# Chunk attention of the first block: heads taken in pairs, step by step, with the products spread between the steps

## Chip, cores and metric

The kernel runs on one core of a Trainium2 chip. The metric is the device time of one execution in microseconds (us), the median of the runs.

## What is computed

512 tokens of width 1024 pass through a block of two layers and then a second block. The part that matters here is the second layer of the first block, cut to its core:

```
hn = rms_norm(h, kv_norm_g)
k, v = hn @ w_k, hn @ w_v                      # 16 heads of 64
q = rms_norm(h, g[0]) @ w_q
s = einsum('bcqhd,bckhd->bchqk', q, k_band)    # 64-token chunks, own chunk and 8 before
s = s * (HEAD_DIM ** -0.5) + relative_bias(rel_table)
s = where(valid, s, NEG_INF)
p = softmax(s, axis=-1)
o = einsum('bchqk,bckhd->bcqhd', p, v_band)
m = o @ w_o
h = h + rms_norm(m, g[1])
```

With 512 tokens a query sees every earlier chunk and its own.

## The kernel before, in words

Activations stand feature-major, 8 tiles of 128 features by 512 tokens. Each weight matrix comes in units: 128 rows by 1024 columns, which are 8 tiles of 128x128, the weights of 128 output features. SyncE loads a unit into one of four slots of `RAW`. GpSimd splits it into a high part `WH` and a rest `WL` (L292, L295). Activations are split likewise (`XH`/`XL`, `HH`/`HL`). A tile of a product is then three matmuls (`three_passes`, L333 to L335), a product 24, and its result stands in one PSUM bank of 512 columns. The counts `weights_split`, `units_done` and `evacuated` order it: a unit waits for its split weights and a free bank, GpSimd for the slot, VectorE for the result.

The attention layer has 8 units for V, 16 for K and Q, 8 for the out product. V goes first, token-major. Then come four K/Q products (two of K, two of Q) for the first four heads, and four rounds of four heads.

In a round (`attention_round`, one on each engine) a block n is one head and one query tile t of 128 tokens, which needs 128(t+1) keys: n = 8a + 4hh + t for head hh of pair a. TensorE, at block n, does the scores of n (L463, K of 64 features, so 64 rows of the array), the transposes of the probabilities of n-2 (L473), the values of n-3 (L484, output to 64 partitions), and in the first three rounds, for n < 12, two tiles of one of the next round's K/Q products (`piece`). These are plain fp32 matmuls. VectorE adds the bias (L1192), takes the negated maximum (L1099), and later the reciprocal of the sum (L1105) and the scaling (L1106). ScalarE does the exponential with its sum (L733), copies the transposes out of PSUM (L744), and stages each round: it copies K, Q and V of the two pairs to `KP`, `QP` and `VP` (L799 to L801), since the rounds are a loop with register addresses and the next K and Q overwrite `KQ`. Outputs of a pair go to `VT` (L804).

Round 4 is the same without products. Then ScalarE copies the eight output tiles from `VT` to `HH` (L815), VectorE takes the rest into `HL` (L1209), and the eight out products run: three together, tile by tile as the parts come, then five.

The scores of block n stand in bank 4 + n % 2, the transposes in 6 + n % 2, the values of pair a in bank a, and K/Q products in banks 2 and 3.

Of the kernel before, what the change touches and what calls it, by code (L numbers as in the profile page):

```python
# [27 lines left out]
P = 128  # L28
SEQ = 512
D = 1024  # L30
# [87 lines left out]
def program(nc, xT, weights, gains, cols, lng, lnb, bs, wsT, rel, pos, ident_d, decay, pT, out):  # L118
    with ExitStack() as ctx:
# [31 lines left out]
        KQ = at("KQ", 152, [P, 4, SEQ])  # L151
        MGH = at("MGH", 144, [P, DT, SEQ], F32R)
# [11 lines left out]
        PTB = at("PTB", 194, [P, 2, SEQ])  # L164
        ROT = at("ROT", 188, [P, 4, SEQ])
# [57 lines left out]
        oh_ready = sem("att_high_ready")  # L223

# [82 lines left out]
        def _(pe):  # L307
# [224 lines left out]
            for xh, xl in ((XH, XL), (XH, XL), (HH, HL), (HH, HL)):  # L532
                product(DT, xh, xl)
            pe.wait_ge(evacuated, bank.now() + SLOTS)
            outs = Count(oh_ready)

            def first_round(ahead):
                attention_round(lambda a: KP[:, a, :], lambda a, hh, k: VP[:, a, k, hh * HD:hh * HD + HD],
                                outs, ahead)
            with loop(pe, 3, [(st, 2), (sr, 16), (pr, 16), (pt, 16), (outs, 2), (split, 4), (bank, 4)]) as i:  # L540
                first_round(((XH, XL), (HH, HL)))
            first_round(None)
            pe.wait_ge(oh_ready, outs.now())
            hr.next(DT)
            products(HH, HL, hr)
# [89 lines left out]
        def _(act):  # L635
# [36 lines left out]
            def branch_squares(first, tables=False):  # L672

                ev.n = SLOTS + first
                for t in range(DT):
                    act.wait_ge(evacuated, ev.next())
                    square(M[:, t, :])
# [106 lines left out]
            def load_bias(i, a):  # L784


                h = bass.ds(i * 4 + 2 * a, 2)
                to = slice(2 * a, 2 * a + 2)
                act.dma_start(BIAS[CH:P, to, :], rel[CH:P, h, :]).then_inc(in_bias[a], 16)
                act.dma_start(BIAS[0:CH, to, 0:SEQ - CH], rel[0:CH, h, 0:SEQ - CH]).then_inc(in_bias[a], 16)  # L790

            def pair_of(i, a):

                return VT[:, :, bass.ds(i * 256 + a * P, P)]

            def stage_pairs(i):
                act.wait_ge(evacuated, ev.next(4))
                for a in range(2):
                    S.activation(KP[:, a:a + 1, :], KQ[:, a:a + 1, :], ACT.Copy)  # L799
                    S.activation(QP[:, a:a + 1, :], KQ[:, 2 + a:3 + a, :], ACT.Copy)  # L800
                    S.activation(VP[:, a, :, :], pair_of(i, a), ACT.Copy).then_inc(staged, 1)  # L801

            def output(i, a):
                S.activation(pair_of(i, a), PS[:, a, :].rearrange("p (t n) -> p t n", t=TT), ACT.Copy)\  # L804
                 .then_inc(oh_ready, 1)
            load_bias(0, 0)
            load_bias(0, 1)
            ev.n = SLOTS + FIRST["att_kq"]
            with loop(act, 3, [(mx, 16), (td, 16), (pv, 16), (ev, 4)]) as i:
                attention_round(i, stage_pairs, output, lambda a: load_bias(i + 1, a))  # L810
            attention_round(3, stage_pairs, output)
            act.wait_ge(units_done, FIRST["att_out"] + SLOTS)
            act.wait_ge(oh_ready, DT)
            for f in range(DT):
                S.activation(HH[:, f, :].rearrange("p (t n) -> p t n", t=TT), VT[:, :, f * P:f * P + P], ACT.Copy)\  # L815
                 .then_inc(xh_ready, 1)
            branch_squares(FIRST["att_out"])
            stat()

            pre_norm([(G_FFN1, XH)], FIRST["ffn_a1"], hn)  # L820
# [102 lines left out]
        def _(dve):  # L923
# [265 lines left out]
            def add_bias(n, dst, src):  # L1189
                if n % 8 == 0:  # L1190
                    dve.wait_ge(in_bias[n // 8], bias_in[n // 8].next(32))
# [333 lines left out]
```

## Time and profile before

| | us |
|---|---|
| median of 3 runs | 2806.67 |
| lowest, highest | 2802.98, 2808.89 |
| span of the profiled execution | 2797.4 |
| TensorE matmul busy | 2563.7 (92%) |
| VectorE busy | 1393.3 (50%) |
| ScalarE busy | 545.4 (19%) |
| GpSimd busy | 1779.9 (64%) |
| mean granted TensorE clock | 0.936 |

The profile's own execution is known by its span, from the first to the last instruction; the times of the runs include what lies around it. A busy share is an average over stages: the attention layer is one stage among 17, so it is read by its own stretch, which runs from 635.5 to 937.0 us, with round 1 from 658.5, round 2 from 715.6, round 3 from 775.1, round 4 from 836.2 to 889.3, and then the out products. The granted clock is a share of 2.4 GHz: 1.00 is that level, 0.50 is 1.2 GHz. A time of a matmul in the timeline includes its way through the array, so its cost in a row of matmuls is read from start to start.

### The profile page before, as it was taken

What the parts mean: (1) busy time and instruction counts of PE and PEld (TensorE: products, weight loads), DVE (VectorE), ACT (ScalarE), POOL (GpSimd) and SP (SyncE); (2) the same over time, 40 slices, a digit from 0 to 9 for tenths busy, and PEclk for the clock granted to TensorE, in tenths of its full rate; (3) what the DMA queues carried; (4) which work ended last, traced back from release to release, by engine and by line L of the source; (5) the groups of instructions that cost most, each with busy time, mean ns of one, the idle gap of its engine ahead of it and who ended that gap; (6) DMA issues with size and microseconds to landing.
All of it is one profiled execution on the core that took longest, in us unless ns stands there. A gap on an engine that the chain in (4) does not pass through costs nothing.

```text
span 2797.4 us, 31291 instructions
## 1 busy us (share of the span) xinstructions
PE 2563.7 (92%) x10766; PEld 2002.8 (72%) x10766; DVE 1393.3 (50%) x1682; ACT 545.4 (19%) x972; POOL 1779.9 (64%) x827
## 2 busy tenths in 40 slices
PE   6789999979999799997899998788989998999987
PEld 5667888856555688886688886456567887888875
DVE  4665433563543634437633237789435237423366
ACT  2122110121332211111211012320322112101022
POOL 6657787845320687786588776464015877887865
PEclk9999999989996999999899999898579999999998
DMA  4222333322110233332233322122002332333322
GB/s 161 76 66 83 98 98 97 92 66 82 52 51 0 68 106 96 92 103 79 63 98 97 96 84 77 53 75 60 0 27 60 97 101 78 103 98 90 99 74 68
DMA packets 64795, 221.40 MB, mean 79 GB/s; under 512 B 7504, under 2 KB 9680, under 8 KB 64592
## 3 DMA queue, kind: packets, MB, share of 16 engines
q1 hardware_dynamic: 59184, 208.17, 25.3%
q10 hardware_dynamic: 5536, 12.19, 1.4%
q8 instruction: 52, 0.85, 0.1%
q14 instruction: 23, 0.19, 0.0%
HBM read 218.23 MB, written 2.10 MB: 79 GB/s over the span
## 4 chain that ended last, share of the span: by engine, by line
PE 77%; DVE 16%; issue 3%; ACT 2%; POOL 1%; ACTq 0%; DMA 0%; DVEq 0%; POOLq 0%
PE PS L333 21%; PE PS L334 21%; PE PS L335 21%; PE PS L403 3%; PE PS L463 3%; PE PS L484 3%; DVE SS L956 2%; DVE XL L964 2%; PE PS L473 2%; DVE RI L974 1%; PE PS L573 1%; POOL WH L292 1%; DVE T L985 1%; DVE MK L1279 1%; POOL WL L295 1%
## 5 line engine op out<-in xcount | busy, mean ns | idle before, releaser
L292 POOL TENSOR_TENSOR WH<-RAW,ONES 128x1024 fp32r<-128x1024 f32 (+3 forms) x411 | 791.2, 1925 | 959.0 <-PE PS L335 867.1
L295 POOL TENSOR_TENSOR WL<-RAW,WH 128x1024 fp32r<-128x1024 f32 (+3 forms) x411 | 993.5, 2417 | 32.3
L333 PE MATMUL PS<-XH,WH 128*128 128x512 f32 x1816 | 729.0, 401 | 80.6 <-DVE XL L964 27.6
L334 PE MATMUL PS<-XL,WH 128*128 128x512 f32 x1816 | 715.9, 394 | 0.0
L335 PE MATMUL PS<-XH,WL 128*128 128x512 f32 x1816 | 714.8, 394 | 0.0
L333 PEld LDWEIGHTS PS<-XH,WH 128*128 128x128 f32 x1816 | 347.0, 191 | 183.3 <-issue 71.1
L333 PE MATMUL PS<-HH,WH 128*128 128x512 f32 x1056 | 416.3, 394 | 13.7 <-DVE M L996 10.9
L334 PE MATMUL PS<-HL,WH 128*128 128x512 f32 x1056 | 413.2, 391 | 0.0
L335 PE MATMUL PS<-HH,WL 128*128 128x512 f32 x1056 | 413.0, 391 | 0.0
L335 PEld LDWEIGHTS PS<-XH,WL 128*128 128x128 f32 x1816 | 346.3, 191 | 74.1
L334 PEld LDWEIGHTS PS<-XL,WH 128*128 128x128 f32 x1816 | 347.0, 191 | 70.6 <-issue 1.4
L1010 DVE TENSOR_TENSOR HL<-T,HH 128x512 f32 x108 | 227.7, 2108 | 152.8 <-ACT HH L702 108.2
L333 PEld LDWEIGHTS PS<-HH,WH 128*128 128x128 f32 x1056 | 199.6, 189 | 60.0 <-issue 12.1
L335 PEld LDWEIGHTS PS<-HH,WL 128*128 128x128 f32 x1056 | 199.5, 189 | 42.1
L334 PEld LDWEIGHTS PS<-HL,WH 128*128 128x128 f32 x1056 | 199.6, 189 | 40.6
L1042 DVE TENSOR_TENSOR M<-PS,M 128x512 f32 x80 | 55.4, 692 | 329.7 <-PE PS L335 329.7
L699 ACT ACTIVATE T<-T 128x512 f32<-128x512 f32 x64 | 40.4, 632 | 496.9 <-DVE T L1017 496.9
L403 PE MATMUL PS<-WH,XH 128*128 128x512 f32 x192 | 83.7, 436 | 57.9 <-DVE XL L964 32.2
L956 DVE TENSOR_TENSOR SS<-SS,T 128x512 f32<-128x512 f32 x91 | 109.5, 1203 | 26.9 <-ACT T L658 26.9
L1027 DVE TENSOR_TENSOR T<-PS,RI 128x512 f32<-128x512 f32 x44 | 30.4, 690 | 182.9 <-PE PS L335 182.9
L964 DVE SCALAR_TENSOR_TENSOR XL<-H,GAIN,XH 128x512 fp32r<-128x512 f32 x64 | 92.4, 1444 | 0.0
L733 ACT ACTIVATE PB<-PB,NM 128x128 f32<-128x128 f32 (+1 forms) x96 | 53.9, 561 | 195.1 <-DVE NM L1099 194.6
(190 smaller groups left out, 2413.6 us busy)
## 6 DMA issues: line engine op xcount, KB each, us to landing
RAW<-in_weights SPq DMA_DIRECT2D x379, 512.0 KB, 3.5
RAW<-in_weights SPq DMA_DIRECT2D x16, 384.0 KB, 3.2
H<-in_xT ACTq DMA_DIRECT2D x8, 256.0 KB, 8.8
BIAS<-in_rel ACTq DMA_DIRECT2D x8, 256.0 KB, 3.4
RAW<-in_weights SPq DMA_DIRECT2D x8, 256.0 KB, 2.7
out<-R ACTq DMA_DIRECT2D x8, 256.0 KB, 2.1
BIAS<-in_rel ACTq DMA_DIRECT2D x8, 224.0 KB, 3.8
DECAY<-in_decay ACTq DMA_DIRECT2D x1, 1024.0 KB, 5.0
```

Of the source, the lines that this page charges most:

```text
L292: nc.gpsimd.tensor_tensor(WH[:, slot, 0:w], raw, ONES[:, 0:1].to_broadcast([P, w]), ALU.mult).then_inc(high_split, 1)
L295: nc.gpsimd.tensor_tensor(WL[:, slot, 0:w], raw, WH[:, slot, 0:w].bitcast(F32), ALU.subtract).then_inc(weights_split, 1)
L333: nc.tensor.matmul(PS[:, bank_, :], WH[:, slot, w], xh[:, k, :], start=(k == 0), stop=False)
L334: nc.tensor.matmul(PS[:, bank_, :], WH[:, slot, w], xl[:, k, :], start=False, stop=False)
L335: return nc.tensor.matmul(PS[:, bank_, :], WL[:, slot, w], xh[:, k, :], start=False, stop=stop)
L403: last = nc.tensor.matmul(PS[:, (first + j) % SLOTS, :], x[:, k, tok], wt[:, slot, w], start=(k == 0 and n == 0), stop=(k == DT - 1 and n ...
L463: nc.tensor.matmul(PS[:, 4 + n % 2, 0:n_of(t)], QP[r, a, t * P:t * P + P], k_of(a)[r, 0:n_of(t)], start=True, stop=True).then_inc(s_done, 1)
L473: last = nc.tensor.transpose(PS[:, 6 + n % 2, k * P:k * P + P], PB[:, n % 3, k * P:k * P + P], IDENT[:])
L484: last = nc.tensor.matmul(PS[hh * HD:hh * HD + HD, a, t * P:t * P + P], v_of(a, hh, k), PTB[:, n % 2, k * P:k * P + P], start=(k == 0), st ...
L956: V.tensor_tensor(SS[:], SS[:], T[:, slot, :], ALU.add).then_inc(ss_ready, 1)
L964: V.scalar_tensor_tensor(dl[:, t, :], H[:, t, :], gain(g, t), dh[:, t, :].bitcast(F32), ALU.mult, ALU.subtract).then_inc(ready, 1)
L1010: V.tensor_tensor(HL[:, f, :], T[:, src:src + 1, :], HH[:, f, :].bitcast(F32), ALU.subtract).then_inc(h_ready, 1)
```

## The change

The rounds and their loops go. 32 steps s = 4p + t are written out, each for both heads of pair p and query tile t. TensorE does the scores of step s, two tiles, the transposes of step s-1, two tiles, the values of step s-1. The tiles come from one list: the 16 K/Q units, ordered K, Q, K, Q by pair, then 21 tiles of the first three out units. 18 tiles stand ahead of step 0. K goes to bank 2 and Q to bank 3.

The staging copies go: scores read K and Q from `KQ`, which holds two pairs, and values read V from `VT`. VectorE adds the bias and takes the negated maximum in one `tensor_tensor_reduce`. A pair's output is split straight from PSUM: ScalarE writes the high part `OH`, VectorE the rest `OL`. The out product's result goes to `M2` in place of `M`, in banks shifted by two. `load_bias` is per pair.

```diff
+            def kq_tile(j):
+                n, k = kq0 + j // DT, j % DT
+                xh, xl = (XH, XL) if n % 2 == 0 else (HH, HL)
+                if k == 0:
+                    pe.wait_ge(weights_split, n + 1 + SLOTS)
+                    pe.wait_ge(evacuated, n + 3)
+                last = three_passes(2 + n % 2, n % SLOTS, slice(k * P, k * P + P), xh, xl, k, k == DT - 1)
...
+            def out_tile(j):
+                n, k = (out0 + j % 2, j // 2) if j < 2 * DT - 2 else (out0 + 2, j - 2 * DT + 2)
...
+                pe.wait_ge(o_low, k + 1)
+                out_high(n, k)
+                out_low(n, k)
...
+            def pair_scores(s):
+                p, t = divmod(s, TT)
+                if t == 0:
+                    pe.wait_ge(evacuated, kq0 + 2 * p + 2 + SLOTS)
+                if s:
+                    pe.wait_ge(x_done, 2 * s)
+                for hh in range(2):
+                    r = slice(hh * HD, hh * HD + HD)
+                    nc.tensor.matmul(PS[:, 4 + hh, 0:n_of(t)], KQ[r, 2 + p % 2, t * P:t * P + P],
+                                     KQ[r, p % 2, 0:n_of(t)], start=True, stop=True).then_inc(s_done2, 1)
+            def pair_transposes(s):
+                t = s % TT
+                for hh in range(2):
+                    pe.wait_ge(p_done, 2 * s + hh + 1)
+                    if s:
+                        pe.wait_ge(pt_done, 2 * s - 1 + hh)
+                    for k in range(t + 1):
+                        last = nc.tensor.transpose(PS[:, 6 + hh, k * P:k * P + P],
+                                                   PROB[:, s % 2, hh, k * P:k * P + P], IDENT[:])
...
+            def pair_values(s):
+                p, t = divmod(s, TT)
+                pe.wait_ge(pt_done, 2 * s + 2)
+                if t == 0 and p >= 2:
+                    pe.wait_ge(o_low, p - 1)
+                for k in range(t + 1):
+                    for hh in range(2):
+                        last = nc.tensor.matmul(PS[hh * HD:hh * HD + HD, p % 2, t * P:t * P + P],
+                                                VT[:, k, (2 * p + hh) * HD:(2 * p + hh) * HD + HD],
+                                                PROBT[:, hh, k * P:k * P + P], start=(k == 0), stop=(k == t))
...
+            for j in range(2 * DT + 2):
+                filler(j)
+            for s in range(steps + 1):
+                j = 2 * DT + 2 + 4 * s
+                if s < steps:
+                    pair_scores(s)
+                filler(j)
+                filler(j + 1)
+                if s:
+                    pair_transposes(s - 1)
+                filler(j + 2)
+                filler(j + 3)
+                if s:
+                    pair_values(s - 1)
+            pe.wait_ge(o_high, DT)
+            for n in range(out0, out0 + 3):
+                out_high(n, DT - 1)
+            pe.wait_ge(o_low, DT)
+            for n in range(out0, out0 + 3):
+                out_low(n, DT - 1).then_inc(units_done, 1)
...
+            def high_output(p):
+                act.wait_ge(pv_done2, 2 * TT * (p + 1))
+                S.activation(OH[:, p, :], PS[:, p % 2, :], ACT.Copy).then_inc(o_high, 1)
...
+            for s in range(DT * TT):
+                p, t = divmod(s, TT)
+                if t == 1 and p:
+                    high_output(p - 1)
+                if s:
+                    probs_out(s - 1)
+                for hh in range(2):
+                    c = s % 2 * 2 + hh
+                    act.wait_ge(x_done, 2 * s + hh + 1)
+                    x = PROB[:, s % 2, hh, 0:n_of(t)]
+                    S.activation(x, x, ACT.Exp, bias=NMX[:, c:c + 1], scale=-1.0,
+                                 accum_out=SUMX[:, c:c + 1]).then_inc(e_done, 1)
...
+            def low_output(p):
+                dve.wait_ge(o_high, p + 1)
+                t = slice(p * P, p * P + P)
+                V.tensor_tensor(OL[:, :, t], PS[:, p % 2, :].rearrange("p (t n) -> p t n", t=TT),
+                                OH[:, p, :].rearrange("p (t n) -> p t n", t=TT).bitcast(F32), ALU.subtract)\
+                 .then_inc(o_low, 1)
...
+                for hh in range(2):
+                    c = s % 2 * 2 + hh
+                    dve.wait_ge(s_done2, 2 * s + hh + 1)
+                    if s >= 2:
+                        dve.wait_ge(t_done2, 2 * s - 3 + hh)
+                    V.tensor_tensor_reduce(PROB[:, s % 2, hh, 0:n], PS[:, 4 + hh, 0:n],
+                                           BIAS[:, p % 2 * 2 + hh, SEQ - n:SEQ],
+                                           -1.0, 3e38, ALU.add, ALU.min, NMX[:, c:c + 1]).then_inc(x_done, 1)
+                if t == 1 and p < DT - 1:
+                    take_k(p + 1)
+                if t == 3 and p < DT - 1:
+                    take_q(p + 1)
+                if t == 1 and p:
+                    low_output(p - 1)
+                for hh in range(2):
+                    c = s % 2 * 2 + hh
+                    x = PROB[:, s % 2, hh, 0:n]
+                    dve.wait_ge(e_done, 2 * s + hh + 1)
+                    link(V.reciprocal(RECX[:, c:c + 1], SUMX[:, c:c + 1]))
+                    V.tensor_scalar(x, x, RECX[:, c:c + 1], None, ALU.mult).then_inc(p_done, 1)
```

How the instructions now stand. First TensorE, before: blocks 4 and 5 of round 1 (L463 scores, L473 transposes, L484 values, L333 to L335 a tile of a product).

```order
L463 MATMUL PS<-T 128x128 [waits scores_read]
L473 MATMUL PS<-IDENT,PB 128x128 [waits probs_t_ready,probs_ready]
L473 MATMUL PS<-IDENT,PB 128x128 x2
L484 MATMUL PS<-PTB,VP 64x128 [waits probs_t_ready]
L484 MATMUL PS<-PTB,VP 64x128
L341 REGISTER_ALU
L333 MATMUL PS<-HH,WH 128x512 [waits evacuated,weights_split]
```

TensorE in the change, steps 2 and 3 of pair 0 (L602 scores, L612 transposes, L623 values, L345 to L347 a tile).

```order
L623 MATMUL PS<-PROBT,VT 64x128 [waits pair_probs_t_ready]
L623 MATMUL PS<-PROBT,VT 64x128
L602 MATMUL PS<-KQ 128x384 [waits pair_biased]
L602 MATMUL PS<-KQ 128x384
L345 MATMUL PS<-HH,WH 128x512
```

```order
L612 MATMUL PS<-IDENT,PROB 128x128 [waits pair_probs_t_ready,pair_probs_ready]
L612 MATMUL PS<-IDENT,PROB 128x128
L612 MATMUL PS<-IDENT,PROB 128x128 [waits pair_probs_t_ready,pair_probs_ready]
L612 MATMUL PS<-IDENT,PROB 128x128
L345 MATMUL PS<-HH,WH 128x512
```

Scores, transposes and values of one head stood together between two pairs of tiles. Now values and scores stand together, each for two heads, and the transposes apart from them with a pair of tiles on either side.

VectorE in a round before, one block of 256 columns and the one behind it:

```order
L1192 TENSOR_TENSOR PB<-PS,BIAS 128x256 [waits probs_transposed,scores_done]
L1099 TENSOR_REDUCE NM<-PB 128x1 [waits scores_read]
L1105 RECIPROCAL REC<-SUM 128x1 [waits exp_done]
L935 REGISTER_ALU
L1106 TENSOR_SCALAR PB<-PB,REC 128x128 [waits dve_self]
```

and in the change, a step with t = 1 of the second pair (L1329 bias and maximum, L1302 K of the next pair, L1314 the rest of the pair before):

```order
L1329 ISA PROB,NMX<-PS,BIAS 128x256 [waits pair_transposed,pair_scores_done]
L1329 ISA NMX 128x1
L1329 ISA PROB,NMX<-PS,BIAS 128x256 [waits pair_transposed,pair_scores_done]
L1329 ISA NMX 128x1
L1302 TENSOR_TENSOR KQ<-PS,RI 128x512 [waits units_done]
L1314 TENSOR_TENSOR OL<-PS,OH 128x4x128 [waits pair_high_ready]
L1342 RECIPROCAL RECX<-SUMX 128x1 [waits pair_exp_done]
L1343 TENSOR_SCALAR PROB<-PROB,RECX 128x256 [waits dve_self]
```

The scaling now follows the same step's exponential, behind the K product's pick-up and the output's rest, and not the next block's addition and maximum.

## Rows read from the trace of the kernel before

**Rows 1.** The page: busy us (share of the span) and instructions of each engine.

```profile
PE 2563.7 (92%) x10766; PEld 2002.8 (72%) x10766; DVE 1393.3 (50%) x1682; ACT 545.4 (19%) x972; POOL 1779.9 (64%) x827
```

**Rows 2.** Busy time by stage: start:end and length us; busy us (instructions) by engine, granted clock, DMA.

```profile
635.50:658.50 23.00, 21.98 (x96) 17.88 (x96) 4.83 (x8) 0.26 (x1) 17.23 (x9) 1.00 0.32 94
658.50:715.60 57.10, 54.33 (x248) 34.21 (x248) 28.73 (x68) 19.43 (x55) 20.62 (x10) 1.00 0.24 71
715.60:775.10 59.50, 56.79 (x250) 36.29 (x249) 28.73 (x68) 21.56 (x57) 17.24 (x8) 0.95 0.18 52
775.10:836.20 61.10, 56.13 (x248) 35.80 (x248) 28.73 (x68) 23.69 (x62) 17.27 (x8) 0.97 0.17 51
836.20:889.30 53.10, 51.96 (x152) 28.67 (x152) 23.05 (x64) 17.68 (x53) 0.00 (x0) 0.52 0.00 0
889.30:937.00 47.70, 45.38 (x192) 37.13 (x192) 17.94 (x23) 9.29 (x16) 28.04 (x12) 0.96 0.20 55
```

**Rows 3.** Timeline of TensorE in round 1: start us, length us, instruction, count.

```profile
674.26 0.48 PE L463 MATMUL PS<-T 64*128 64x128 f32 x2
674.67 0.55 PE L473 MATMUL PS<-IDENT,PB 128*128 128x128 f32 x3
675.15 0.65 PE L484 MATMUL PS<-PTB,VP 128*64 128x128 f32 x4
675.73 0.50 PE L333 MATMUL PS<-HH,WH 128*128 128x512 f32 x1
...
677.32 0.70 PE L463 MATMUL PS<-T 64*128 64x256 f32 x2
...
684.62 1.12 PE L463 MATMUL PS<-T 64*128 64x512 f32 x2
685.67 0.44 PE L473 MATMUL PS<-IDENT,PB 128*128 128x128 f32 x2
686.04 0.43 PE L484 MATMUL PS<-PTB,VP 128*64 128x128 f32 x2
686.40 0.50 PE L333 MATMUL PS<-HH,WH 128*128 128x512 f32 x1
...
687.99 0.37 PE L463 MATMUL PS<-T 64*128 64x128 f32 x1
```

**Rows 4.** Busy time in two stretches at the end of round 2.

```profile
765.00:770.00 5.00, 2.80 (x13) 1.27 (x12) 3.39 (x9) 2.40 (x7) 0.00 (x0) 0.88 0.45 134
770.00:775.00 5.00, 5.00 (x23) 4.01 (x22) 0.00 (x0) 0.65 (x2) 0.00 (x0) 0.50 0.23 61
```

**Rows 5.** Groups by shape, VectorE (rounds 1 to 3, then round 4), ScalarE: count, busy, mean.

```profile
L1106 DVE TENSOR_SCALAR PB<-PB,REC 128x512 f32<-128x512 f32 x12 | 11.3, 939 | 0.4
...
L1192 DVE TENSOR_TENSOR PB<-PS,BIAS 128x512 f32<-128x512 f32 x12 | 8.3, 692 | 18.3 <-PE PS L463 18.3
...
L1105 DVE RECIPROCAL REC<-SUM 128x1 f32<-128x1 f32 x48 | 7.4, 154 | 1.1 <-ACT PB L733 1.1
...
L1106 DVE TENSOR_SCALAR PB<-PB,REC 128x512 f32<-128x512 f32 x4 | 1.9, 486 | 0.1
...
L733 ACT ACTIVATION_READ_ACCUMULATOR PB<-PB,NM 128x1 f32 x48 | 9.0, 187 | 0.0
L733 ACT ACTIVATE PB<-PB,NM 128x512 f32<-128x512 f32 x12 | 8.7, 722 | 30.3 <-DVE NM L1099 30.3
...
L744 ACT ACTIVATE PTB<-PS 128x512 f32<-128x512 f32 x11 | 6.4, 580 | 2.8 <-PE PS L473 2.8
```

**Rows 6.** Timeline at the handover to the out products.

```profile
890.04 2.19 ACT L815 ACTIVATE HH<-VT 128x512 fp32r<-128x512 f32 x4
...
891.54 0.62 PE L333 MATMUL PS<-HH,WH 128*128 128x512 f32 x1 [2.31 <-DVE HL L1209]
```

**Rows 7.** Timeline of VectorE at the end of the V product.

```profile
634.57 2.07 DVE L1174 TENSOR_SCALAR VT<-PS,RT 128x512 f32<-128x512 f32 x3 [23.83 <-PE PS L403]
```

**Rows 8.** Groups of GpSimd, 640 to 940 us.

```profile
L295 POOL TENSOR_TENSOR WL<-RAW,WH 128x1024 fp32r<-128x1024 f32 x23 | 56.4, 2454 | 1.8
```

More of the change, by code:

```diff
@@ L531, in _ @@
             pe.wait_ge(h_ready, hr.next(DT))
[L532 to L545, printed above, removed]
+            kq0 = FIRST["att_kq"]
+            out0 = FIRST["att_out"]
+            def kq_tile(j):
[5 more added lines that the diff above has]
+                last = three_passes(2 + n % 2, n % SLOTS, slice(k * P, k * P + P), xh, xl, k, k == DT - 1)
+                if k == DT - 1:
+                    last.then_inc(units_done, 1)
@@ new lines, in _ @@
+            steps = DT * TT
+            for j in range(2 * DT + 2):
[13 more added lines that the diff above has]
+            pe.wait_ge(o_high, DT)
@@ new lines, in _ @@
+            for n in range(out0, out0 + 3):
[3 more added lines that the diff above has]
+                out_low(n, DT - 1).then_inc(units_done, 1)
+            split.n, bank.n = out0 + 3 + SLOTS, out0 + 3
+            for n in range(out0 + 3, out0 + DT):
+                pe.wait_ge(weights_split, split.next())
+                pe.wait_ge(evacuated, bank.next())
+                for k in range(DT):
+                    out_high(n, k)
+                    last = out_low(n, k)
+                last.then_inc(units_done, 1)
@@ L782, in _ @@
             stat(token_major=True)
[L784 to L817, printed above, removed]
+            def load_bias(p):
+                h = slice(2 * p, 2 * p + 2)
+                to = slice(p % 2 * 2, p % 2 * 2 + 2)
+                act.dma_start(BIAS[CH:P, to, :], rel[CH:P, h, :]).then_inc(in_bias[p % 2], 16)
+                act.dma_start(BIAS[0:CH, to, 0:SEQ - CH], rel[0:CH, h, 0:SEQ - CH]).then_inc(in_bias[p % 2], 16)
@@ L1194, in next_kq @@
-            def next_kq(i, n):
-                if n in (1, 5, 9, 13):
-                    if n == 1:
-                        dve.wait_ge(staged, st.next(2))
-                    dve.wait_ge(units_done, done.next())
-                    take_kq(n // 4, PS[:, 2 + n // 4 % 2, :])
-            for n in range(4):
-                take_kq(n, unit())
-            with loop(dve, 3, [(sd, 16), (ex, 16), (td, 16), (me, 16), (st, 2), (done, 4)]
-                      + [(x, 32) for x in bias_in]) as i:
-                attention_round(i, add_bias, next_kq)
@@ L1206, in _, with take_k @@
[L1206 to L1212 removed]
+            def take_k(p):
+                dve.wait_ge(units_done, done.next())
+                V.tensor_tensor(KQ[:, p % 2, :], PS[:, 2, :], RI[:], ALU.mult).then_inc(evacuated, 1)
@@ L1440, in lay_out @@
     token_major(i["w_v"])
-    for f in range(0, DT, 2):
-        for w in (i["w_k"], i["b_w_q"][0]):
-            columns(w, f)
-            columns(w, f + 1)
+    for f in range(DT):
+        columns(i["w_k"], f)
+        columns(i["b_w_q"][0], f)
     feature_major(i["b_w_o"][0])
```

105 lines of the change are left out of this document (74 added, 31 removed).

## The prediction

> **What bounds the kernel now.** I read the stretch first through the busy time by stage [rows 2], because the page's totals [rows 1] average over stages with different limits. The block that changes runs from the first K/Q product at 635.5 us to the pick-up of the eighth out product at 937.0: 301.5 us. The reader should see three things in rows 2. First, TensorE is busy nearly everywhere, so other engines matter only where it waits. Second, rounds 1 to 3 take 57.1, 59.5 and 61.1 us with four products in each, and round 4 takes 53.1 us with none. Third, the granted clock is 0.52 in round 4: TensorE stands at its 1.2 GHz level while it has only attention to do.
>
> Next the order of time on TensorE inside round 1 [rows 3]. From one head's scores at 674.26 to the next head's at 687.99 are 13.73 us. Eight weight tiles lie in it. A tile is three matmuls; a product of eight tiles is 24, and 192 tiles are the 24 products of this block. Two tiles stand from 675.73 to 677.32, 1.59 us. The first four products, 96 such matmuls, take 21.98 us [rows 2], of which 0.2 is the end of the last, so one follows the other after 0.227 us, a tile takes 0.68, and 0.22 us of the 1.59 is the switch between kinds of work. One head's attention is thus 13.73 - 5.46 = 8.27 us. The rows split it. Scores of 128 columns take 0.41, of 512 columns 1.05: 0.20 fixed and 0.213 per 128 columns. Transposes: 0.37 for two, 0.48 for three: 0.155 fixed, 0.107 each. Values: 0.36 for one key tile, 0.58 for two: 0.155 fixed, 0.213 each. Over t = 0 to 3 there are ten tiles of each, so a head needs 2.93 + 1.69 + 2.75 = 7.37 us, and four switches 0.88.
>
> Sixteen heads of 7.37 us, the 48 switches of rounds 1 to 3 (10.6 us) and 192 tiles (130.8 us) make 259 us. The other 42 us are waits and low clock: a granted clock of 0.88 and then 0.50 at the end of round 2, where the last quarter of a round has no tiles [rows 4]; round 4; staging copies at the start of rounds; and the handover, in which ScalarE copies the heads' outputs again from 890.04 and the first out product starts at 891.54 [rows 6].
>
> **The change, part by part.** In the new order, a step is one query tile of two heads: scores of both, two tiles, transposes of the step before, two tiles, values of the step before. 18 tiles come ahead, 131 are spread over 33 steps, and the last 43 follow.
>
> Tiles: all 192 remain, 192 x 0.681 = 130.8 us, and now nearly all attention has tiles beside it. Filler makes 10.9 us of about 25.6 us per pair (43%), against 5.46 of 13.73 (40%) in the stretch of rows 3, where the clock is 1.00. I cost the clock at full. Round 4's low clock, the tails and the handover go.
>
> Attention, per pair of heads: scores 4 x 0.20 fixed and 20 x 0.213 = 5.06; transposes 4 x 0.155, a second semaphore wait which I put at 0.06, and 20 x 0.107 = 3.00; values 4 x 0.155 and 20 x 0.213 = 4.88; eight switches 1.76. Together 14.7, times eight 117.6 us.
>
> Start: the first K/Q product now goes to the third bank and waits for the third copy of V instead of the first. VectorE takes 0.69 us for each [rows 7], so 1.3 us later.
>
> End: after the last values ScalarE copies a pair's output (0.6, as in its copies of 512 columns [rows 5]), six matmuls with the high part run beside VectorE's subtraction (0.7), then three and five products. 0.75 us of it is idle.
>
> Sum without anything side by side in the array: 1.3 + 130.8 + 117.6 + 0.75, and 0.2 to the pick-up, are 250.7 us, 50.8 less than 301.5.
>
> Side by side: the rows call the scores 64*128 and the values 128*64. Each uses half of the array, and before, two of different halves never stood next to each other. Now they do: head 0 and head 1 use other rows for scores and other columns for values, in other banks or partitions. The trace shows no such neighbours, so I bound the gain. Below: nothing, as the values of one head follow each other at 0.213 us. Above: half the streaming of scores and values, 8 x 2 x 4.26 / 2 = 34.1 us. In between lies a mechanism from rows 3: every such matmul is two instructions (x2, x4, x6), and starts are in order. Then of a score pair's four instructions only the two in the middle overlap, and a quarter is saved, 8.5 us. Of values, which alternate, 4(t+1) slots become 2(t+1)+1: 24 for 40, saving 13.7 us. I take these 22.2 us, since the two halves share neither operand rows nor output and the engine already loads the next weights under a running matmul; it is the weakest term, and both ends stay in the range.
>
> The Trainium skill (TensorEngine Tiling (Array Packing), Key Properties) says that different tiles can run in parallel, but also that changing the tiling mode drains the array. No row here shows the first; the fixed 0.155 to 0.20 us at each change of shape agrees with the second.
>
> VectorE: the addition (692 ns at 512 columns [rows 5]) and the maximum behind it become one pass with a read-out. Its price is unseen: between 0.69 us, the addition alone, and 1.4, two passes. Per pair VectorE has some 11 us of work in 25, so this is off the path. Latency: in a step with 512 columns, from the scores' end, ScalarE must first copy the step before's transposes (until about 3.0 us), then runs two exponentials of 0.83 (722 ns, of which the 187 ns read-out hides part), and VectorE's reciprocal (154 ns) and scaling (486 ns in round 4) end at 5.4. TensorE comes to the transposes after three pairs of tiles, transposes and values of t = 2 and scores of t = 0: 4.77 + 0.88 + 1.43 + 0.63 = 7.7 us, with overlap 7.1. The scaling can be late: 939 ns in the mean at 512 columns, while GpSimd splits weights in passes of 2.4 us [rows 5, 8].
>
> The Trainium skill (SBUF — State Buffer, Who interferes with whom) says that VectorE's two-port mode and GpSimd lock each other out for a whole instruction. By that a scaling waits up to 2.5 us, until 7.9, and each step that meets it stalls by up to 0.8.
>
> From the row's mean of 939 ns I put 1.5 us in all for such stalls. The bias loads, the unrolled instructions in place of a loop of three rounds, and the new split of the output (which replaces eight copies and eight subtractions) hide behind tiles and cost nothing; without that cover the split costs 1.3 us per pair. GpSimd needs 4.4 us a product and gets 13 or more; of the last five it splits 4.4 against TensorE's 5.4.
>
> Forecast: 50.8 + 22.2 - 1.5 = 71.5 us gained. The profiled span is 2797.4 us, 9.3 under the median of the runs, 2806.7; 2726 of span, and **2735 us** as a median.
>
> **Rivals.**
> A, no overlap in the array: gains 50.8, 2756 us. For it: every row of one head runs in sequence. Against: those rows all share a half.
> B, latency takes over: the fused pass costs two passes (1.4 us more for two heads) and most scalings wait out a pass of GpSimd (up to 2.4 us more, 1.2 in the mean), so with overlap and 1.7 us of slack each of the 24 wider steps stalls 0.9 us. 22 us are given back, 2757 us. Against: the slack of 2.3 us, 1.7 with overlap.
> C, slower: the clock falls to 1.2 GHz although tiles are spread, since the longest stretch without a tile (values t = 2, scores t = 3: 1.4 + 1.9 us) recurs each pair. At half clock the streaming of 131 tiles (89 us) and of attention (85 us) doubles: 174 us more, 123 slower, 2930 us. It turns the sign once more than 50.8 / 174 = 29% of the interleaved work runs low. For it: rows 2 and 4. Against: clock 1.00 throughout rows 3 at 40% filler.
> D, the gain does not appear, because the tiles in the steps wait for one another's banks or weights: within 6 us, 2801 to 2812.
>
> **Numbers.** Forecast 0.50, A 0.32, B 0.07, C 0.05, D 0.06. Faster by over 0.2% (5.6 us, about what a measurement of this kernel can tell from no change): forecast, A, B and a third of D, 0.91. Within: 0.03. Slower: C and the rest of D, 0.06. The range reaches from 2718 (overlap by a full half, 2722, and fixed costs a little smaller) to 2764 (A, and 0.25 us more at each of 32 steps).
>
> **What would show it.** The block from first K/Q product to last out product: 230 us if right, 250 for A. Granted clock 1.00 over all of it. Two scores of 512 columns start to next start in 1.5 us with overlap, 1.9 without. Values of t = 3 for two heads about 1.1 against 1.9. TensorE's waits for probabilities under 3 us in all; for the first K/Q product 1.3 us later. I am wrong in kind if the clock drops inside the steps, or if waits on VectorE or ScalarE exceed 20 us.

## The result, and the profile after

| | before | after |
|---|---|---|
| median of the runs, us | 2807.55 (4 runs: 2802.98 to 2808.89) | 2712.22 (4 runs: 2711.17 to 2713.16) |
| span of the profiled execution, us | 2797.4 | 2709.9 |
| mean granted TensorE clock | 0.936 | 0.942 |

The ratio is 0.9668, 95% interval 0.9657 to 0.9680: 3.3% faster, 95.3 us by the medians. The forecast had 71.5 us and 2735, with a range from 2718 to 2764. So the direction was right and the time lies under the range.

The page of the changed kernel, busy time in us, where [rows 1] stood before:

```profile
PE 2488.0 (92%) x10766; PEld 1963.4 (72%) x10766; DVE 1386.7 (51%) x1682; ACT 523.5 (19%) x938; POOL 1779.3 (66%) x827
```

TensorE has the same number of matmuls, 10766, and is 76 us less busy. The busy time by stage (columns as in [rows 2]): the whole block, then the tiles ahead of step 0, pair 0, pair 1.

```profile
638.10:845.90 207.80, 206.70 (x1184) 147.13 (x1184) 122.97 (x297) 70.00 (x207) 97.92 (x45) 1.00 0.24 71
...
638.10:650.60 12.50, 12.41 (x54) 10.06 (x54) 2.25 (x4) 0.00 (x0) 7.74 (x4) 1.00 0.24 60
650.60:668.80 18.20, 18.17 (x103) 12.34 (x102) 12.34 (x32) 6.54 (x22) 10.04 (x6) 1.00 0.28 87
668.80:689.10 20.30, 20.29 (x126) 13.88 (x124) 13.79 (x36) 8.21 (x25) 8.48 (x5) 1.00 0.26 76
```

The clock is at full (1.00) over the whole block, TensorE is busy for 206.7 of 207.8 us, and the block is 207.4 us from the start of its first matmul (638.19) to the end of its last (845.58); before it was 301.3 (635.47 to 936.77). The end is taken here as the last start (845.35, and 936.54 before) plus the 0.23 us from one such matmul to the next. Against the profiled spans, 87.5 us: the block starts 2.7 later, is 93.9 shorter, and what follows it takes 3.7 longer (1864.3 for 1860.6).

Timeline of TensorE, pair 1 (start us, length us, instruction, count), where [rows 3] stood before:

```profile
668.77 0.49 PE L602 MATMUL PS<-KQ 64*128 64x128 f32 x4
669.20 0.50 PE L345 MATMUL PS<-XH,WH 128*128 128x512 f32 x1
...
670.77 1.25 PE L612 MATMUL PS<-IDENT,PROB 128*128 128x128 f32 x8
671.78 0.47 PE L345 MATMUL PS<-XH,WH 128*128 128x512 f32 x1
...
673.34 1.09 PE L623 MATMUL PS<-PROBT,VT 128*64 128x128 f32 x16
674.37 0.70 PE L602 MATMUL PS<-KQ 64*128 64x256 f32 x4
675.00 0.50 PE L345 MATMUL PS<-XH,WH 128*128 128x512 f32 x1
...
676.50 0.38 PE L612 MATMUL PS<-IDENT,PROB 128*128 128x128 f32 x2
676.63 0.48 PE L345 MATMUL PS<-HH,WH 128*128 128x512 f32 x1
...
678.20 0.44 PE L623 MATMUL PS<-PROBT,VT 128*64 128x128 f32 x4
678.57 0.92 PE L602 MATMUL PS<-KQ 64*128 64x384 f32 x4
679.42 0.50 PE L345 MATMUL PS<-HH,WH 128*128 128x512 f32 x1
...
680.91 0.83 PE L612 MATMUL PS<-IDENT,PROB 128*128 128x128 f32 x4
681.49 0.48 PE L345 MATMUL PS<-HH,WH 128*128 128x512 f32 x1
...
683.06 0.66 PE L623 MATMUL PS<-PROBT,VT 128*64 128x128 f32 x8
683.65 1.13 PE L602 MATMUL PS<-KQ 64*128 64x512 f32 x4
684.71 0.50 PE L345 MATMUL PS<-HH,WH 128*128 128x512 f32 x1
...
686.20 0.82 PE L612 MATMUL PS<-IDENT,PROB 128*128 128x128 f32 x6
686.78 0.47 PE L345 MATMUL PS<-XH,WH 128*128 128x512 f32 x1
...
688.34 0.88 PE L623 MATMUL PS<-PROBT,VT 128*64 128x128 f32 x12
689.14 0.49 PE L602 MATMUL PS<-KQ 64*128 64x128 f32 x4
```

A pair takes 689.14 - 668.77 = 20.37 us. Read start to next start: scores of *both* heads take 0.43, 0.63, 0.85, 1.06 us for 128 to 512 columns, and one head's alone took 0.41 and 1.05 in [rows 3]. Values of both heads take 0.37, 0.59, 0.80 and 1.03 for one to four key tiles. The second head costs nothing in either. Transposes of both heads take 0.13, 0.58, 0.58, 1.01 for 2, 4, 6, 8 blocks.

The end of the block, same view:

```profile
814.38 1.09 PE L623 MATMUL PS<-PROBT,VT 128*64 128x128 f32 x16
816.20 0.50 PE L565 MATMUL PS<-OH,WH 128*128 128x512 f32 x1 [0.72 <-ACT OH L907]
```

The idle time there is 0.72 us, for 0.75 in the forecast. VectorE and ScalarE by shape, from 650 to 820 us (columns as in [rows 5]):

```profile
L1343 DVE TENSOR_SCALAR PROB<-PROB,RECX 128x512 f32<-128x512 f32 x16 | 22.2, 1388 | 0.6
...
L930 ACT ACTIVATE PROB<-PROB,NMX 128x512 f32<-128x512 f32 x16 | 11.4, 721 | 0.0
L1329 DVE CUSTOM_DVE_ANT_0 PROB<-PS,BIAS 128x512 f32<-128x512 f32 x16 | 10.4, 689 | 6.4 <-PE PS L602 6.4
...
L1329 DVE DVE_READ_ACCUMULATOR2_ANT NMX<- 128x1 f32 x64 | 5.2, 82 | 0.0
```

The fused pass takes 689 ns, as long as the addition alone (692), plus a read-out of 82. The scaling takes 1388 ns in the mean, longer than before (939).

### The profile page after: what moved, and what is told of

Its sections match the earlier page's. It is cut to its first block, busy times and chain, and to the rows that moved or that the text cites. A ratio compares the mean times of both kernels' runs of the same rounds, so it can differ in the third digit from the quotient of the medians.

```text
span 2709.9 us, 30992 instructions
## 1 busy us (share of the span) xinstructions
PE 2488.0 (92%) x10766; PEld 1963.4 (72%) x10766; DVE 1386.7 (51%) x1682; ACT 523.5 (19%) x938; POOL 1779.3 (66%) x827
## 4 chain that ended last, share of the span: by engine, by line
PE 77%; DVE 17%; issue 3%; ACT 2%; POOL 1%; DMA 0%; DVEq 0%; ACTq 0%; POOLq 0%
PE PS L345 22%; PE PS L347 21%; PE PS L346 21%; PE PS L415 3%; DVE SS L1075 2%; DVE XL L1083 2%; PE PS L475 1%; PE PS L496 1%; DVE RI L1093 1%; DVE MK L1412 1%; DVE TOP L1411 1%; PE PS L685 1%; PE PS L602 1%; PE PS L623 1%; POOL WH L304 1%
## 5 line engine op out<-in xcount | busy, mean ns | idle before, releaser
L345 PE MATMUL PS<-XH,WH 128*128 128x512 f32 x1816 | 730.9, 402 | 79.9 <-DVE XL L1083 27.4
L347 PE MATMUL PS<-XH,WL 128*128 128x512 f32 x1816 | 716.2, 394 | 0.0
L345 PEld LDWEIGHTS PS<-XH,WH 128*128 128x128 f32 x1816 | 347.4, 191 | 182.5 <-issue 72.3
L347 PEld LDWEIGHTS PS<-XH,WL 128*128 128x128 f32 x1816 | 346.8, 191 | 74.2
L345 PE MATMUL PS<-HH,WH 128*128 128x512 f32 x992 | 390.0, 393 | 8.1 <-DVE M L1115 8.1
L346 PE MATMUL PS<-HL,WH 128*128 128x512 f32 x992 | 387.1, 390 | 0.0
L347 PE MATMUL PS<-HH,WL 128*128 128x512 f32 x992 | 387.0, 390 | 0.0
L345 PEld LDWEIGHTS PS<-HH,WH 128*128 128x128 f32 x992 | 186.8, 188 | 55.9 <-issue 18.0
L347 PEld LDWEIGHTS PS<-HH,WL 128*128 128x128 f32 x992 | 186.8, 188 | 39.1
L346 PEld LDWEIGHTS PS<-HL,WH 128*128 128x128 f32 x992 | 186.9, 188 | 37.9
L415 PEld LDWEIGHTS PS<-WH,XH 128*128 128x128 f32 x192 | 39.9, 208 | 73.2 <-issue 29.6
```

Source lines behind the costliest of these rows:

```text
L345: nc.tensor.matmul(PS[:, bank_, :], WH[:, slot, w], xh[:, k, :], start=(k == 0), stop=False)
L346: nc.tensor.matmul(PS[:, bank_, :], WH[:, slot, w], xl[:, k, :], start=False, stop=False)
L347: return nc.tensor.matmul(PS[:, bank_, :], WL[:, slot, w], xh[:, k, :], start=False, stop=stop)
L415: last = nc.tensor.matmul(PS[:, (first + j) % SLOTS, :], x[:, k, tok], wt[:, slot, w], start=(k == 0 and n == 0), stop=(k == DT - 1 and n ...
```

## The experiments

Every kernel was run beside the kernel before on the same chip; medians. "Block" is as above. All but one edit the changed kernel; the idle tiles edit the kernel before.

**One head's values after the other's.** Is it the alternation that lets the values overlap?

```diff
-                for k in range(t + 1):
-                    for hh in range(2):
+                for hh in range(2):
+                    for k in range(t + 1):
```

> The change, but the values of a step are issued all of head 0 and then all of head 1, where they alternate. In the profile of the change the values of both heads take as long as one head's alone (16 matmul instructions of t = 3 in 1.03 us from start to next start). Theory 1, the array's halves run side by side only for instructions that stand next to each other: the two heads overlap at one place per step, the step at t = 3 goes from 1.03 to about 1.75 us, and the time rises by some 14 us. Theory 2, the engine looks far ahead and fills the free half whatever the order: no change, within 2 us.

Measured: 2717.77 us (2714.3 to 2719.8, 4 runs), ratio 0.969 [0.9674, 0.9706]; block 211.5. Its timeline at the start of pair 1, with the values of t = 2 and t = 3 of pair 0:

```profile
668.81 1.14 PE L623 MATMUL PS<-PROBT,VT 128*64 128x128 f32 x12
669.88 0.49 PE L602 MATMUL PS<-KQ 64*128 64x128 f32 x4
...
674.18 1.58 PE L623 MATMUL PS<-PROBT,VT 128*64 128x128 f32 x16
675.69 0.70 PE L602 MATMUL PS<-KQ 64*128 64x256 f32 x4
```

Values of t = 2 take 1.07 us (0.80 when alternating) and of t = 3 1.51 (1.03), while t = 0 and 1 stay at 0.37 and 0.59. In sequence they would be 1.44 and 1.87. So neither theory holds whole: head 1 starts before head 0 is done, but only by so much. With 2 or 4 instructions of head 0 ahead nothing is lost, with 6 and 8 it is 0.27 and 0.48, some 2.5 and 4.5 instructions of 0.107. The single starts in the trace say where the limit lies. At t = 3 head 1's first instruction starts at 674.675, 6 ns behind the fifth of head 0's eight, and head 0's last three start later, at 674.778, 674.887 and 674.996. At t = 2 it is the third of six, again with three to come. So head 1 gets past three waiting instructions of head 0, whole matmuls among them, and not past more: with the one that has just started, that is a group of four.

**Values in turns of two key tiles.** The test of that reading: four instructions of one head, then four of the other.

```diff
-                for k in range(t + 1):
-                    for hh in range(2):
+                for hh, k in [(h, k) for first in range(0, t + 1, 2) for h in range(2)
+                              for k in range(first, min(first + 2, t + 1))]:
```

> The change, but the values of a step are issued in turns of two key tiles (four matmul instructions) per head, where the change alternates after each key tile (two instructions). With all of head 0 first, the values cost 0.26 us more at t = 2 and 0.48 more at t = 3, as if head 1 could start only when about four matmul instructions of head 0 are left. If that is how far the engine looks ahead: turns of four instructions lose nothing, the values take 0.81 and 1.03 us as in the change, and the time is the same within 1 us. If every change from head to head costs something: values between 0.81 and 1.07 (t = 2), 1.03 and 1.51 (t = 3), 2 to 4 us slower.

Measured: 2711.51 us (2708.1 to 2713.4, 4 runs), 0.9668 [0.9653, 0.9683]; values of t = 2 0.81 and of t = 3 1.07 us. At t = 3 that is 0.05 over the change, 0.4 us in the whole block (207.8 us): groups of four instructions overlap all but fully.

**Scores in turn.** Head 1's scores wait until head 0's are out.

```diff
+                    if hh:
+                        pe.wait_ge(s_done2, 2 * s + 1)
```

> The change, but head 1's scores wait for the end of head 0's. Theory 1, overlap of scores is worth their whole streaming of one head (8 x 10 x 0.213 = 17 us): the time rises by 17 us and by 32 drains and waits of 0.2 to 0.3 us, together 23 to 27 us, and the time from one start of scores to what follows has a slope of 0.43 us per 128 columns, where it has 0.21. The rival, overlap of a quarter only as in the prediction: 8.5 and the drains, 15 to 18 us, and what else came beyond the prediction lies elsewhere.

Measured: 2735.87 us (2735.2 to 2740.4, 4 runs), 0.9759 [0.9743, 0.9775]; block 231.5. That is 23.7 over the change. Scores of t = 0 to 3 now take 0.96, 1.38, 1.81, 2.24 us. Per 128 columns that is 0.427, twice the 0.213 of the change, and the fixed part has grown by 0.33, which is the price of the wait itself.

**Both in turn.** The same with values: head outside, key tile inside, and a wait between heads.

```diff
+                for hh in range(2):
+                    if hh:
+                        pe.wait_ge(pv_done2, 2 * s + 1)
```

> The change without any overlap in the array: head 1's scores wait for head 0's scores, and head 1's values for head 0's values. Theory 1: 34 us of streaming come back and 64 drains and waits of 0.2 to 0.3 us, 47 to 53 us in all, and what is left of the gain against the kernel before, 42 to 48 us, is that of tiles spread over all steps, of the clock and of the missing handover (the prediction had 50.8 for these). Rival, the pairing itself gave little and the spread nearly all: the time rises by under 30 us.

Measured: 2760.54 us (2758.6 to 2763.9, 4 runs), 0.9846 [0.983, 0.9862]; block 256.8. The scores and, further on, the values of t = 3 of pair 0 in its timeline, the values with what follows them:

```profile
665.70 2.30 PE L604 MATMUL PS<-KQ 64*128 64x512 f32 x4
...
678.08 2.23 PE L627 MATMUL PS<-PROBT,VT 128*64 128x128 f32 x16
680.24 1.45 PE L604 MATMUL PS<-KQ 64*128 64x256 f32 x4
```

48.3 us over the change. Values take 0.86, 1.29, 1.73, 2.16, so 0.43 per key tile for 0.22, and 0.275 more fixed. 32 x (0.33 + 0.275) = 19.4 us of the block are the two waits. Without them a block with no overlap is 256.8 - 19.4 = 237.4: 63.9 us of the gain need no overlap. The other 30.0 are the overlap, 33.5 us by the rows of pair 1 (below), less the stalls at the transposes, 3.1 us, which the change has and this run has not (its transposes take 0.14, 0.35, 0.57 and 0.79).

**The out tiles after the attention.** The last steps keep their order but lose their tiles.

```diff
-                elif j < 2 * DT * DT + 3 * (DT - 1):
-                    out_tile(j - 2 * DT * DT)
...
+            for j in range(3 * (DT - 1)):
+                out_tile(j)
```

> The change, but the 21 tiles of the out product that stand in steps 27 to 32 come behind the attention, so that its last five steps have nothing beside them. If tiles beside attention are what keeps the clock up and covers the waits: TensorE waits for probabilities at each of these steps (2 to 4 us each, 10 to 18 us in all), the granted clock falls to 0.50 in the stretch, and the time rises by 12 to 25 us. If the spread is worth little here: under 4 us.

Measured: 2719.79 us (2718.6 to 2723.2, 4 runs), 0.9701 [0.9685, 0.9717]; 7.6 over the change, between the two expectations. Busy time by stage (granted clock third from the end), then the timeline of TensorE. The last tile beside the attention ends before 788, and the next starts at 808.27:

```profile
790.00:795.00 5.00, 2.16 (x19) 1.64 (x18) 3.59 (x10) 2.12 (x8) 1.93 (x1) 0.89 0.35 103
795.00:800.00 5.00, 4.57 (x30) 2.41 (x26) 2.97 (x13) 2.17 (x8) 0.00 (x0) 0.77 0.00 2
797.50:808.00 10.50, 7.69 (x66) 4.48 (x66) 6.75 (x25) 6.81 (x20) 0.00 (x0) 1.00 0.01 2
```

```profile
792.27 1.25 PE L610 MATMUL PS<-IDENT,PROB 128*128 128x128 f32 x8 [2.15 <-DVE PROB L1343]
794.20 1.98 PE L621 MATMUL PS<-PROBT,VT 128*64 128x128 f32 x16 [0.69 <-ACT PROBT L916]
```

Without tiles TensorE waits for the chain of VectorE and ScalarE: 2.15 us once, and 0.43 to 0.69 before every later values and some transposes. The clock dips for a few microseconds only, behind the wait of 2.15 us. From 797.5 to 808.0 it is back at 1.00, with attention alone on TensorE and TensorE busy for 7.69 of 10.5 us. So paired attention needed no tiles there to stay at full clock, and the tiles in the last steps are worth 7 us, mostly as cover for latency.

**Addition and maximum as two passes.** ScalarE's exponential then takes the negated maximum as it is, without its scale of -1.

```diff
-                    V.tensor_tensor_reduce(PROB[:, s % 2, hh, 0:n], PS[:, 4 + hh, 0:n],
-                                           BIAS[:, p % 2 * 2 + hh, SEQ - n:SEQ],
-                                           -1.0, 3e38, ALU.add, ALU.min, NMX[:, c:c + 1]).then_inc(x_done, 1)
+                    link(V.tensor_tensor(PROB[:, s % 2, hh, 0:n], PS[:, 4 + hh, 0:n],
+                                         BIAS[:, p % 2 * 2 + hh, SEQ - n:SEQ], ALU.add))
+                    V.tensor_reduce(NMX[:, c:c + 1], PROB[:, s % 2, hh, 0:n], axis=AX, op=ALU.max,
+                                    negate=True).then_inc(x_done, 1)
```

> The change, but with the addition and the maximum as two instructions on VectorE, as in the kernel before (the step with 512 columns has 1.4 us more on VectorE, the sum over 64 blocks is about 32 us of VectorE). If latency has slack in a step, as the prediction says: within 3 us of the change. If the fused pass is what keeps TensorE fed (rival B of the prediction): 10 to 25 us slower, with TensorE waiting for the scores' reading or for probabilities.

Measured: 2713.14 us (2711.9 to 2717.0, 4 runs), 0.968 [0.9664, 0.9696]; block 207.9. No difference: the fused pass is worth nothing here, because VectorE is off the path.

**Idle tiles in round 4 of the kernel before.** Is it attention alone that lowered the clock in [rows 2]? This kernel does 32 tiles more than it must, and their result is used by nobody.

```diff
+                    if idle and n < 16:
+                        for k in range(2):
+                            three_passes(2 + n % 2, 0, slice(k * P, k * P + P), XH, XL, 0, True)
```

> The kernel before, with 32 tiles (96 matmuls, two tiles behind each block) added to round 4, whose results nobody reads: 21.8 us of work more at full clock and 3.5 us of switches. If the low clock of round 4 comes from having attention alone on TensorE: the granted clock is 1.00 there, the round goes from 53.1 us to 55 to 57, and the whole is 2 to 4 us slower although it does 25 us more. If the clock is low for another reason: 40 us slower or more.

Measured: 2806.31 us (2800.5 to 2810.6, 10 runs), 1.0012 of the kernel before [1.0002, 1.0021]. Busy time by stage, round 4:

```profile
838.70:842.00 3.30, 3.29 (x8) 2.30 (x8) 0.58 (x2) 1.92 (x5) 0.00 (x0) 0.50 0.02 5
842.00:870.00 28.00, 28.00 (x123) 17.17 (x123) 12.69 (x36) 8.43 (x26) 0.00 (x0) 1.00 0.00 1
870.00:894.80 24.80, 24.80 (x120) 15.53 (x118) 9.80 (x26) 7.45 (x21) 0.00 (x0) 1.00 0.00 0
```

The clock is at 0.50 until the first tiles are done, at full from 842.0 on, and stays there. Round 4 takes 56.1 us with 25 us of work more (32 tiles of 0.68 and 16 switches of 0.22), so its attention takes 31 us for the 53.1 of [rows 2]. The lack of tiles cost 22 us, and the useful tiles that the change puts there get that for nothing. Not all of it need be the clock: tiles also cover waits, which the run with the out tiles last shows at full clock, and no run has round 4 without tiles at full clock.

**The first K and Q in banks 0 and 1.** VectorE reads these two products from there.

```diff
-                    pe.wait_ge(evacuated, n + 3)
-                last = three_passes(2 + n % 2, n % SLOTS, slice(k * P, k * P + P), xh, xl, k, k == DT - 1)
+                    pe.wait_ge(evacuated, n + 1 if n < kq0 + 4 else n + 3)
+                last = three_passes(n % 2 if n < kq0 + 2 else 2 + n % 2, n % SLOTS, slice(k * P, k * P + P), xh, xl, k, k == DT - 1)
```

> The change, but the first K and Q products go to banks 0 and 1, so that the first one waits for the first copy of V instead of the third. Expected: the idle time ahead of the first K product falls from 2.25 to 0.94 us, and the time by 1.3 us, which lies at the edge of what the runs can tell. If something else holds the start (weights, the activations' parts): no change in that idle time.

Measured: 2710.0 us (2708.2 to 2713.3, 4 runs), 0.9664 [0.9648, 0.9681]. Timeline of TensorE, this kernel and then the change:

```profile
636.52 0.47 PE L345 MATMUL PS<-XH,WH 128*128 128x512 f32 x1 [0.94 <-DVE VT L1293]
```

```profile
638.19 0.47 PE L345 MATMUL PS<-XH,WH 128*128 128x512 f32 x1 [2.25 <-DVE VT L1293]
```

The wait is 1.31 us shorter, the 1.3 of the forecast. By medians 2.2 us, in overlapping ranges.

**The scaling on ScalarE.** VectorE only takes the reciprocal, and counts it in `r_done`.

```diff
+                    act.wait_ge(r_done, 2 * s + hh + 1)
+                    x = PROB[:, s % 2, hh, 0:n_of(t)]
+                    S.activation(x, x, ACT.Copy, scale=RECX[:, c:c + 1]).then_inc(p_done, 1)
...
-                    V.tensor_scalar(x, x, RECX[:, c:c + 1], None, ALU.mult).then_inc(p_done, 1)
```

> The change, but the probabilities are scaled by ScalarE instead of VectorE (64 more ScalarE instructions of 0.3 to 0.6 us, 64 fewer on VectorE, which took 1.39 us at 256 and 512 columns while GpSimd was at work). If VectorE's scaling waits for GpSimd's passes and TensorE then waits for it: the transposes of t = 1 go from 0.58 to 0.36 us and of t = 3 from 1.01 to 0.79, 3 us in all, unless ScalarE, which must also copy the transposes, becomes late. If ScalarE becomes late: waits of TensorE for transposed probabilities, 3 to 15 us slower.

Measured: 2712.11 us (2707.1 to 2715.6, 4 runs), 0.9672 [0.9652, 0.9692]; block 203.6, 3.8 less than in the change. Transposes take 0.14, 0.36, 0.57 and 0.79 us, 0.22 less than in the change for t = 1 and t = 3: those were the stalls on the scaling, 7 x 0.44 = 3.1 us, as the last pair of the change has none. But the rest after the block takes 1868.3 us, 4.0 more, and the time does not move.

**Both of these, and the change again,** five rounds each.

> The change with both edits that each took a wait away: the first K and Q product in banks 0 and 1, and the scaling on ScalarE. If the two gains add: 1.3 us from the start, and about 2.5 us from the transposes of t = 1 and t = 3, together 2 to 4 us faster than the change run beside it. If ScalarE now becomes late somewhere: no gain or a loss, and waits for transposed probabilities on TensorE.

> The changed kernel itself, once more, as what the kernel with both edits is compared with on the same chip: 2709 to 2714 us.

Measured: both 2707.37 us (2703.5 to 2710.5, 5 runs), 0.9648 [0.9635, 0.9661]; the change again 2714.45 (2706.7 to 2716.1, 5 runs), 0.9671 [0.9657, 0.9684]. The change again lies 0.5 us above what was expected of it. The first is the best version seen, 7 us better by medians, but the runs overlap, so do the intervals, and the profiled spans differ by 2.4 us only (2708.7 and 2711.1). In its trace the block starts 3.8 us earlier and is 3.8 shorter than in the trace of the change again, and the rest takes 5.3 longer (1869.5 for 1864.2). The stages after the block differ in granted clock at their starts; this is the same stretch of 12 us after the block, the change and then the kernel before:

```profile
858.60:870.60 12.00, 11.07 (x36) 8.92 (x37) 11.86 (x19) 6.04 (x10) 0.00 (x0) 0.71 0.01 4
```

```profile
949.80:961.80 12.00, 11.62 (x42) 8.97 (x43) 11.82 (x19) 5.22 (x10) 0.00 (x0) 0.86 0.01 3
```

TensorE gets through 36 matmuls there at 0.71, and 42 at 0.86. The code behind the block is the same in all the edited versions of the change, yet that rest takes from 1860.7 us (values in turns of two, with a mean granted clock of 0.94) to 1869.5 (both edits, 0.93). What decides how much of a gain of a few microseconds is given back later was not settled.

## Why the prediction was right, and where it was wrong

**What bounds the kernel: right.** TensorE did, and still does (206.7 of 207.8 us). That round 4's low clock would go with tiles beside the attention held: 1.00 over the whole block, also in the run with both in turn, and the idle tiles show the price of the bare round, 22 us. That attention alone is what lowers the clock holds only for one head at a time: TensorE was at 0.50 while busy for 50.2 of 51.2 us in round 4 (837.1 to 888.3), and with the out tiles last at 1.00 for 10.5 us of bare paired attention. Whether the second half of the array makes that difference was not tested apart.

One count of the prediction is off, without weight in its sum: rounds 1 to 3 have 39 stretches of tiles (tiles stand behind 12 of the 16 blocks, and eight ahead of them), not 48, so 2.0 us of its 259 belong to the 42 us of waits and low clock.

**The tiles: right.** 16 tiles in pair 1 are 10.90 us; 20.37 less that leaves 9.47 for the attention of a pair. Forecast: 14.7 less 22.2 / 8, or 11.9. Pairs 1 to 6 all take 20.4 us, so pair 1 stands for them, and its rows split the difference:

| per pair, us | forecast | measured |
|---|---|---|
| scores | 5.06 - 1.06 = 4.00 | 2.97 |
| values | 4.88 - 1.71 = 3.17 | 2.79 |
| transposes | 3.00 | 2.30 |
| switches | 1.76 | 1.41 |
| sum | 11.93 | 9.47 |

The switches are what the eight pairs of tiles take over 16 x 0.681. 8 x 2.46 = 19.7 us, and 1.5 of stalls that the forecast had on top (the measured ones are inside the rows), make 21.2 of the 21.1 us by which the block fell short of its forecast (228.5 from first start to last matmul).

**The step that failed first: "starts are in order".** It made a quarter of the scores and 24 slots for 40 of the values. The overlap is full, or all but: 22.2 us and 8 x (1.03 + 0.38) more make 33.5, for an upper end of the bound of 34.1. Scores and values of two heads cost what one head's cost. The four instructions of the two 512-column scores, in the view by source line of the change (shortest, median and longest in ns, first and last start in us):

```profile
L602 PE MATMUL PS<-KQ x4: 589/641/693, 663.3 to 663.8; 64*128 64x512 f32 x4
```

All four have started 0.5 us after the first; one head's two alone are 0.5 apart when the 1.05 us of [rows 3] are halved. With starts held up by head 0's second instruction, the last would start 1 us after the first. The run with values by head shows it without a doubt about the order: all of head 0's matmuls stand ahead there, and head 1's first starts while three instructions of head 0 still wait. The Trainium skill (TensorE: Matmul & The Clock Gate, Part 3: Packing small matmuls — row/col tiling) says that matmuls start and end in program order, with no reordering. The trace of that run does not agree: head 1's first matmul instruction, ninth in the program, starts at 674.675, and head 0's eighth at 674.996. Only for the scores, where two instructions of one head stand beside two of the other, does it stay open whether one is passed over or they are handed over interleaved. The reading of that rule out of [rows 3] was the error: those rows hold no neighbours on different halves, so they could not show a start out of order either. The bound from above was the better guide.

**The second: a fixed 0.155 us for each group of transposes.** In [rows 3] scores stood ahead of them and values behind, of other shapes. In the change they stand between tiles, and both are 128*128. That this is the reason is the likely reading; no run moved the transposes alone. Two blocks cost 0.13 us in all, and with the scaling on ScalarE the four groups are 0.14, 0.36, 0.57 and 0.79: nothing fixed, 0.107 a block. That is 1.86 for the forecast's 3.00, and the forecast's 0.06 for the second semaphore wait is not seen. The switches are cheaper too, perhaps for the same reason: 1.41 us for 1.76.

**Stalls: right in kind, half in size.** 3.1 us for 1.5. The cause is the one named, the scaling held up by GpSimd's passes, and taking it off VectorE removes them. The mean of 1388 ns hides two kinds. Engines in order of time, pair 1, t = 3:

```profile
688.42 2.38 POOL L307 TENSOR_TENSOR WL<-RAW,WH 128x1024 fp32r<-128x1024 f32 x1
688.53 2.55 DVE L1343 TENSOR_SCALAR PROB<-PROB,RECX 128x512 f32<-128x512 f32 x1
...
691.19 0.49 DVE L1343 TENSOR_SCALAR PROB<-PROB,RECX 128x512 f32<-128x512 f32 x1
```

The scaling of head 0 starts 0.11 us behind a pass of GpSimd and ends 0.28 behind its end; head 1's, with no pass beside it, takes 0.49. In pairs 0 to 6 each step of t = 3 has one of 2.55 and one of 0.49, and each of t = 1 one of 2.35 and one of 0.7 to 0.8. At t = 2, with no pass beside them, all take 0.42. These are the same steps whose transposes stall.

**Start and end: right.** 1.3 us by the banks, 0.72 for 0.75. The other 1.4 us by which the block starts later lie in code that the change leaves alone. Executions differ there: the idle time ahead of the block begins at 635.94 in the change and at 635.58 with the first banks, by the two rows above.

**After the block: nothing shown.** The sum left it unchanged, and in the profiled execution it takes 3.7 us more (1864.3). But the run with values in turns of two, with the same code there, takes 1860.7, as the kernel before does (1860.6). So the 3.7 us lie within what executions of one code differ by, and no run ties them to the change.

**Span and median: wrong.** The forecast added 9.3 us for what lies around the span. It is 1.8 us in every run, and the profiled execution of before was shorter than the runs: the 29 executions of before beside the experiments have spans of 2797.6 to 2806.7, and the profiled one had 2797.4. For the change the median lies 2.3 over its profiled span. So the 22.8 us from 2735 down to 2712.2 are 21.1 of block, less 1.4 and 3.7 before and behind it, and 7.0 from this (23.0, with the forecast rounded by 0.2).

**The rivals.** A (no overlap) falls by the timeline, and its 250 us of block with it. Even a kernel without overlap would have been better than A's price, 237.4 us by the runs in turn. B (latency) falls: two passes cost nothing. C (low clock) falls: the longest stretches without a tile stay at 1.00, and even 10.5 us of paired attention without any tile do. But for one head at a time the clock does follow what stands beside the attention, as round 4 with and without tiles shows. D falls: TensorE is busy for 206.7 of 207.8 us.

## What to carry to other kernels

Two small plain fp32 matmuls on different halves of the array, in rows or in columns, cost the time of one here when they stand next to each other in the stream; alternate them, or keep each group to four instructions, and put no semaphore wait between them (0.28 to 0.33 us each, on top of the overlap). Try small work of the full 128*128 shape between other work of that shape: here it cost its streaming alone. Look at single durations where a mean seems long: one scaling of 2.55 us and one of 0.49 need another cure than two of 1.39. When a term has never been seen in a trace, let the two ends of its bound carry more of the range than a mechanism read out of rows that cannot show it; and take the distance from span to run time from several runs, not from one profiled execution.

## What the runs showed that was not expected

- Full overlap of plain fp32 matmuls on two halves: 1.06 us for two scores of 512 columns, 1.03 us for 16 instructions of values.
- Its reach: head 1 starts with three instructions of head 0 still waiting, never more (values by head lose 0.27 and 0.48 us at 6 and 8, nothing at 2 and 4).
- Plain fp32 attention of one head at a time, alone, stands at a granted clock of 0.50 with TensorE busy throughout (50.2 of 51.2 us); two tiles between blocks bring it to 1.00, in the same round of the same kernel. Attention of two heads side by side, alone, ran at 1.00 with TensorE busy for 7.69 of 10.5 us.
- A scaling of VectorE that starts beside a pass of GpSimd lasts until 0.15 to 0.28 us behind the end of that pass (2.55 us at 512 columns for 0.49).
- A block 3.8 us shorter (scaling on ScalarE) left the time where it was: the stages after it took 4.0 us more.
